# Modulation products of a three-part network: from TensorE to GpSimd, during the feed-forward layers

## What is computed

```python
def conv_glu_ffn(x, w_up, conv_w, conv_b, w_down):
    h = causal_depthwise_conv(x @ w_up, conv_w, conv_b)
    gate, val = jnp.split(h, 2, axis=-1)
    return (jax.nn.silu(gate) * val) @ w_down
# first part, twice: h = h + mixer(rmsnorm(h)); h = h + conv_glu_ffn(rmsnorm(h))
# then, for each of the 2 hybrid layers and for both c (latents) and c_ctx (context):
#   mod = silu(c) @ w_mod[layer] + b_mod[layer]     # 1024 -> 3072
```

## Time and profile before

| | |
|---|---|
| device time, median of 3 runs | 2967.27 us (2965.48 to 2967.45) |
| span of the profiled execution | 2965.5 us (its device time 2965.48 us) |
| TensorE matmuls | 2901.6 us busy, 98% |
| TensorE weight loads | 2393.2 us, 81% |
| VectorE | 1477.4 us, 50% |
| ScalarE | 1163.9 us, 39% |
| GpSimd | 146.0 us, 5% |
| mean granted clock of TensorE | 0.997 |
| DMA | 260.98 MB, mean 88 GB/s |

### The profile page before, as it was taken

The page is one execution under the profiler, slowest core; times in us unless marked ns, Lnnn a source line. Parts: engine busy times, 40 slices in busy tenths (PEclk is TensorE's granted clock), DMA queues, the critical chain, the costliest instruction groups (busy, mean ns, idle before and its releaser), DMA issues.

```text
span 2965.5 us, 38348 instructions
## 1 busy us (share of the span) xinstructions
PE 2901.6 (98%) x15438; PEld 2393.2 (81%) x15438; DVE 1477.4 (50%) x2051; ACT 1163.9 (39%) x1856; POOL 146.0 (5%) x199
## 2 busy tenths in 40 slices
PE   9999999999999999999999999999999999999998
PEld 7778888776788887877888788868888788888776
DVE  5655455546463657366252543263455735453454
ACT  5444333526452344146233431173232743341452
POOL 1000000110000000100000300100001000200100
PEclk9999999999999999999999999999999999999999
DMA  5343332331332222210112221311113022321322
GB/s 185 122 158 105 113 128 85 129 130 38 136 107 98 99 87 76 82 54 22 60 43 76 85 68 57 101 60 64 57 64 101 21 82 78 108 91 66 121 75 85
DMA packets 48844, 260.98 MB, mean 88 GB/s; under 512 B 6872, under 2 KB 7904, under 8 KB 24896
## 3 DMA queue, kind: packets, MB, share of 16 engines
q1 hardware_dynamic: 36288, 213.75, 20.8%
q0 software_dynamic: 12416, 45.25, 4.5%
HBM read 250.50 MB, written 4.28 MB: 86 GB/s over the span
## 4 chain that ended last, share of the span: by engine, by line
PE 91%; DVE 4%; ACT 3%; DMA 1%; issue 1%; POOL 0%; SPq 0%; DVEq 0%; ACTq 0%
PE PS L897 15%; PE PS L898 15%; PE PS L899 15%; PE PS L874 7%; PE PS L876 7%; PE PS L875 7%; PE PS L833 3%; PE PS L835 3%; PE PS L834 3%; PE PS L1124 2%; PE PS L1086 1%; PE PS L1197 1%; PE PS L1179 1%; PE PS L1166 1%; PE PS L944 1%
## 5 line engine op out<-in xcount | busy, mean ns | idle before, releaser
L897 PE MATMUL PS<-HHX,WHX 128*128 128x512 f32 (+1 forms) x1440 | 504.6, 350 | 0.4 <-DVE WLX L2409 0.3
L898 PE MATMUL PS<-HL,WHX 128*128 128x512 f32 (+1 forms) x1440 | 503.4, 350 | 0.0
L1680 ACT ACTIVATE WHX<-W 128x2048 fp32r<-128x2048 f32 (+1 forms) x102 | 174.8, 1713 | 560.9 <-DMA W<-in_w 379.2
L899 PE MATMUL PS<-HHX,WLX 128*128 128x512 f32 (+1 forms) x1008 | 350.1, 347 | 0.0
L2409 DVE TENSOR_TENSOR WLX<-W,WHX 128x2048 fp32r<-128x2048 f32 x60 | 137.5, 2292 | 344.9 <-ACT WHX L1680 344.8
L897 PEld LDWEIGHTS PS<-HHX,WHX 128*128 128x128 f32 x1440 | 272.7, 189 | 38.3 <-DVE WLX L2409 1.5
L898 PEld LDWEIGHTS PS<-HL,WHX 128*128 128x128 f32 x1440 | 272.7, 189 | 34.9
L874 PE MATMUL PS<-HH,WH 128*128 128x512 f32 x672 | 261.7, 389 | 0.0
L876 PE MATMUL PS<-HH,WL 128*128 128x512 f32 x672 | 261.7, 389 | 0.0
L875 PE MATMUL PS<-HL,WH 128*128 128x512 f32 x672 | 261.6, 389 | 0.0
L2409 DVE TENSOR_TENSOR WL<-W,WH 128x2048 fp32r<-128x2048 f32 x68 | 155.7, 2290 | 177.8 <-ACT WH L1680 177.7
(11 more groups left out here) (553 smaller groups left out, 5813.8 us busy)
## 6 DMA issues: line engine op xcount, KB each, us to landing
W<-in_w SPq DMA_DIRECT2D x172, 1024.0 KB, 4.8
XC<-in_wm POOLq DMA_DIRECT2D x12, 1024.0 KB, 5.2
H<-in_wm POOLq DMA_DIRECT2D x12, 1024.0 KB, 6.0
W<-in_wb SPq DMA_DIRECT2D x24, 512.0 KB, 3.3
W<-in_w SPq DMA_DIRECT2D x8, 768.0 KB, 4.1
ARENA<-ARENA POOLq DMA_DIRECT2D x32, 128.0 KB, 2.3
ARENA<-mrow SPq DMA_DIRECT2D x12, 256.0 KB, 3.9
PR<-in_nbias POOLq DMA_DIRECT2D x12, 256.0 KB, 3.0
```

The source lines that it names most:

```text
L897: pe.matmul(dst, wh[:, s, c], hi[:, k, t0:t1], start=k == 0, stop=False)
L898: pe.matmul(dst, wh[:, s, c], lo[:, k, t0:t1], start=False, stop=False)
L899: mm = pe.matmul(dst, wl[:, s, c], hi[:, k, t0:t1], start=False, stop=k == kb - 1)
L1680: act.activation(dst[:, s, 0:n], W[:, s, 0:n], ACT.Copy).then_inc(wh_ready[s], 1)
```

## The change

The eight matmuls for each slab go away, with SCW, the zeroing of PSUM and the count `mods`. In their place GpSimd multiplies, in the stage "up" at the head of each feed-forward layer, slabs 0 to 15 (first layer) and 16 to 23 (second layer), one behind the other. For one slab and each of its 8 row blocks it does two multiplications of 128x256 by a per-partition scalar (silu(c), silu(c_ctx)), into the slab's row of MACC or into one of two 128x512 buffers (RST and PR); from the second row block on, an addition of 128x512 sums them. That is 16 multiplications and 7 additions. Each instruction counts `mod_step` up, and GpSimd waits on that count: before the products of row block k (k from 2) for everything issued, before the last addition for everything issued, and before it issues the load of slab i+2 for the whole slab i. The sum over the 128 partitions is left to TensorE: in the third "down" of the first layer and in the second "down" of the second layer it waits until GpSimd has finished the group, and then does one matmul of 512 columns per slab, with a stationary operand of 32 columns out of ONEHOT of which one is all ones (16 and 8 matmuls, four at a time in four column groups). ScalarE copies the rows out, TensorE sums and turns them with four matmuls, VectorE adds `b_mod`, as before but once per group.

```diff
+MOD_GROUPS = (0, 16, MODS)
+    MACC = ARENA[:, split_at + 4 * KT * SLAB + KT * T:][:, 0:16 * 2 * SLAB].rearrange("p (a b) -> p a b", a=16)
+    MODP = PR[:, 0:4 * P]
-    def pe_mod(pe, st, n, done=0):
-            pe.wait_ge(mod_loaded[i % 2], 16 * (i // 2 + 1))
-                    mm = pe.matmul(PS[32 * g:32 * g + MOD_COLS, 4 + i % 2, 0:SLAB], SCW[:, c:c + MOD_COLS],
-                                   mod_slab(i)[:, k, :], start=opens and half == 0, stop=half == 1,
-                                   skip_group_check=True)
-            mm.then_inc(mod_used, 1)
...
+    def mod_steps(slabs):
+        return (3 * KT - 1) * slabs
+    def mod_group(st):
+        if st.kind == "down" and (st.layer, st.step0) == (0, PARTS[0] + PARTS[1]):
+            return 0
+        if st.kind == "down" and (st.layer, st.step0) == (1, PARTS[0]):
+            return 1
+        return None
+    def pool_mod(pool, own, i):
+        row = i - MOD_GROUPS[int(i >= MOD_GROUPS[1])]
+        acc = MACC[:, row, :].rearrange("p (c n) -> p c n", c=2)
+        made = [RST[:, T:2 * T], MODP]
+        pool.wait_ge(mod_loaded[i % 2], 16 * (i // 2 + 1))
+        def product(k):
+            dst = made[k % 2].rearrange("p (c n) -> p c n", c=2) if k else acc
+            wait(pool, mod_step, own.n - (1 if k < 2 else 0))
+            for c in range(2):
+                own.mark(pool.tensor_scalar(dst[:, c, :], mod_slab(i)[:, k, :], SC[:, k, c:c + 1], None, ALU.mult))
+        def add(k):
+            pool.wait_ge(mod_step, own.n - (2 if k + 1 < KT else 0))
+            own.mark(pool.tensor_tensor(acc, acc, made[k % 2].rearrange("p (c n) -> p c n", c=2), ALU.add))
+        product(0)
+        product(1)
+        for k in range(1, KT):
+            if k + 1 < KT:
+                product(k + 1)
+            add(k)
+    def pe_mod_rows(pe, group):
+        first, end = MOD_GROUPS[group:group + 2]
+        pe.wait_ge(mod_step, mod_steps(end))
+        wait(pe, sem("mod_out"), group)
+        for j in range((end - first) // 4):
+            for g in range(4):
+                mm = pe.matmul(PS[32 * g:32 * g + 32, 4, :], ONEHOT[:, 3 - j:3 - j + 32], MACC[:, 4 * j + g, :],
+                               start=j == 0, stop=4 * j + 4 == end - first, skip_group_check=True)
+        mm.then_inc(sem("mod_rows"), 1)
...
     def pe_down(pe, st):
-        if takes_ctx(st):
-            pe_mod_sum(pe, 1, 3)
-        pe_mod(pe, st, min(st.mods, 1))
+        group = mod_group(st)
+        if group is not None:
+            pe_mod_rows(pe, group)
...
         pe_split_unit(pe, st, 0, tile_of(HIDH), tile_of(HIDL), (hid_lo, ready), kb=st.n, slots=(1,))
+        if group is not None:
+            pe_mod_sum(pe, group)
...
     def act_down(act, own, st):
-        if st["mod"] + st.mods == MODS and st.mods:
-            act_mod_out(act, 0, 2, MODS - 1)
+        group = mod_group(st)
+        if group is not None:
+            act_mod_out(act, group)
...
     @block.gpsimd
-            for i in range(st["mod"] + 2, min(st["mod"] + st.mods + 2, MODS)):
-                pool.wait_ge(mod_used, i - 1)
-                if st.kind in ("units", "tok"):
-                    pool.wait_ge(w_ready[1], 16 * (st["it"] + i - st["mod"]))
-                pool.dma_start(mod_slab(i), wm[i, :, :, :]).then_inc(mod_loaded[i % 2], 16)
+            if st.kind == "up" and st.step0 == 0:
+                pool.wait_ge(h_ready, st["hr"])
+                pool.wait_ge(sem("sc_ready"), 1)
+                wait(pool, sem("mod_rows"), st.layer)
+                for i in range(*MOD_GROUPS[st.layer:st.layer + 2]):
+                    pool_mod(pool, own, i)
+                    if i + 2 < MODS:
+                        pool.wait_ge(mod_step, mod_steps(i + 1))
+                        pool.dma_start(mod_slab(i), wm[i + 2, :, :, :]).then_inc(mod_loaded[i % 2], 16)
```

More of the change, by code:

```diff
@@ L152, in plan_stages @@
     norm("H", "load", "mix0_norm")
-    units(["xa", "ga"], at="H", era="even", split=True, first=True, mods=2)
+    units(["xa", "ga"], at="H", era="even", split=True, first=True)
     add("lru", {**full(0, 1, 2, 3, n=2), **free(0, 1, 2, 3, n=2)})
-    units(["cp", "vb", "bp"], at="H", era="even", split=True, mods=3)
-    units(["res", "res"], at="Y", era="even", split=True, final=True, mods=1)
-    norm("H", "res", "ffn_norm0", mods=2)
+    units(["cp", "vb", "bp"], at="H", era="even", split=True)
+    units(["res", "res"], at="Y", era="even", split=True, final=True)
+    norm("H", "res", "ffn_norm0")
     for f in range(2):
@@ L163, in plan_stages @@
             add("down", {"it": 2, "ws": 2, "w8": 4, **full(0, 2, n=2), **free(0, 1, 2, 3, n=2)}, layer=f,
-                n=2 * n, step0=sum(PARTS[:part]), split=True, apart=True, final=part == len(PARTS) - 1,
-                mods=((2, 2, 1), (2, 0, 0))[f][part])
+                n=2 * n, step0=sum(PARTS[:part]), split=True, apart=True, final=part == len(PARTS) - 1)
         if f == 0:
-            norm("H", "down", "mix1_norm", mods=2)
-            units(["u", "q", "k"], at="H", era="odd", split=True, first=True, mods=3)
-            tok(["g", "v"], era="odd", split=True, final=True, mods=1)
+            norm("H", "down", "mix1_norm")
+            units(["u", "q", "k"], at="H", era="odd", split=True, first=True)
+            tok(["g", "v"], era="odd", split=True, final=True)
             add("sgu", {**full(0, 1, 2, 3), **free(0, 1, 2, 3)})
@@ L172, in plan_stages @@
             add("fox", {**full(0, 2, n=8), **free(0, 2, n=8), **full(4, n=16), **free(4, n=16)}, jobs=jobs)
-            assert base["mod"] == MODS_EVEN
-            units(["res", "res"], at="Y", era="odd", split=True, first=True, final=True, mods=1)
-            norm("H", "res", "ffn_norm1", mods=2)
+            units(["res", "res"], at="Y", era="odd", split=True, first=True, final=True)
+            norm("H", "res", "ffn_norm1")
     norm("both", "down", "final_norm")
@@ L682, in pe_mod_sum, with act_mod_out @@
+    def pe_mod_sum(pe, group):
+        pe.wait_ge(sem("mod_out"), group + 1)
+        wait(pe, sem("mod_saved"), group)
+        for b in range(4):
+            mm = pe.matmul(PS[:, 5, 16 * b:16 * b + 16], MODP[:, b * P:(b + 1) * P],
+                           PC[:, PCOL["mod_sum"]:PCOL["mod_sum"] + 16], start=True, stop=True,
                            skip_group_check=True)
         mm.then_inc(sem("mod_summed"), 1)
[L685 to L689, removed]
+    def act_mod_out(act, group):
+        act.wait_ge(sem("mod_rows"), group + 1)
+        wait(act, sem("mod_summed"), group)
+        act.activation(MODP, PS[:, 4, :], ACT.Copy).then_inc(sem("mod_out"), 1)
@@ L691, in dve_mod_save @@
     def dve_mod_save(dve, group):
[L693 to L703, removed]
-                              ALU.add).then_inc(sem("mod_saved"), 1)
+        dve.wait_ge(sem("mod_summed"), group + 1)
@@ L706, in pe_idle, with slabs_of @@
+        i0, i1 = MOD_GROUPS[group:group + 2]
+        def slabs_of(v):
+            return v.rearrange("p (a m c) -> p a m c", m=2, c=2)[:, i0:i1, :, :]
+        new = PS[:, 5, 0:64].rearrange("p (c m a) -> p a m c", m=2, c=2)[:, 0:i1 - i0, :, :]
+        dve.tensor_tensor(slabs_of(MODT[:, :, :, :].rearrange("p a b c -> p (a b c)")), new,
+                          slabs_of(PC[:, PCOL["b_mod"]:PCOL["b_mod"] + 4 * MODS]),
+                          ALU.add).then_inc(sem("mod_saved"), 1)
     def pe_idle(pe, n):
@@ L1735, in act_down @@
             if u == 0:
-                if st["mod"] + st.mods == MODS and st.mods:
-                    act_mod_out(act, 1, 3, MODS)
                 if takes_ctx(st):
@@ L3036, in _ @@
     def _(pool):
+        own = Own(pool, mod_step)
         pool.memset(EPSC[:, 0:1], EPS).then_inc(consts, 1)
@@ L3256, in pad8 @@
         return o
+    mod_sum = np.zeros((P, 16), np.float32)
+    for slab in range(16):
+        mod_sum[32 * (slab % 4) + slab // 4, slab] = 1.0
     ffn = []
```

75 lines of the change are left out of this document (19 added, 56 removed).

## The result

The changed kernel takes 3147.03 us in the median of 4 runs (3143.95 to 3147.68), beside 2967.36 us for the kernel before on the same chip: ratio 1.0604, 95% interval 1.0589 to 1.0619. It is slower by 180 us, where +22 was forecast and the range ended at 3030. The direction was right, the size was not.

A forecast was written before the change was run, and what follows sets the result against it. TensorE, busy 98% of the span, was taken as the bound. Terms -19.8 + 6 + 29 (waiting for GpSimd) + 4 + 1 + 2 gave +22 us on 2967.3, so 2989 us, range 2954 to 3030 us.

The forecast's parts named there:

- Slabs off TensorE, row matmuls on: TensorE's stream: 18 exposed slabs removed, -19.8 us, 24 new matmuls of 512 columns, +6 us; together -13.8 us.
- The multiplication: GpSimd's 128x256 product by a scalar: 0.40 us each, bounds 0.29 and 0.73, 6.4 us a slab.
- the 21: GpSimd's first group: 21 us of its 277 pass under VectorE's time, 12 of waits and issue, 9 of start-up.
- The room and the lock: GpSimd's first group: 325 us from start to deadline, less 98 us lost to VectorE's two-SBUF-input operations, leaves 227 us.
- The waits on its own count: GpSimd waiting for its issued instructions, eight times a slab: 0.2 us each, bounds 0.1 and 0.3, 1.6 us a slab.
- the other count: First group: if VectorE's L2462 operations were locked out too, room shrinks by 64 us and TensorE waits 93 us.
- Group 1: GpSimd's slabs in the second feed-forward layer: 128 us needed in a room of 149, no wait, 21 us to spare.
- VectorE: VectorE's two-input operations delayed by GpSimd in the feed-forward layers: +4 us, bounds 0 and 12.
- The clock: Granted clock falling after TensorE's waits: +1 us for the three norms, +2 us behind the long wait.
- 17 us with little work: Profile stretch before a granted clock of 0.88 over 11 us, read as 1.3 us' worth of work lost.
- The dear multiplication: GpSimd's multiplications cost 0.73 us like a two-input operation; TensorE waits 113 and 21 us: 3096 us, chance 10%.
- VectorE as the bound: Feed-forward layers: VectorE's six two-input operations a unit each wait a whole addition, +33 us besides the wait: 3022 us, 8%.

The follow-up runs named there:

- kernel with the filled norms: Ten matmuls on constants added in each of the three norms that lost slabs, against the changed kernel cut to one column an operation: 2953.58 us.
- kernels with one column: Changed kernel with each GpSimd multiplication and addition working on one column of each half, MACC zeroed once per group: 2958.02 us, ratio 0.9971.
- kernel without reads: Changed kernel with GpSimd's instructions replaced by memsets of about the same time, plus a MACC memset ahead of each group: 3039.79 us.
- paired multiplication: Changed kernel with each row block's two multiplications by a scalar made one two-input multiplication of 128x512: 3016.97 us, ratio 1.0171.
- kernel that follows: Kernel before, with 18 slabs moved to GpSimd using one two-input multiplication per row block, six norm slabs kept on TensorE: 2954.66 us, ratio 0.9961.

## Why the prediction was wrong

The terms can be checked against one point, TensorE's first waiting matmul in the fourth norm (before: 1161.58 us), behind which neither kernel has any of this work. The kernel with the filled norms is there at 1146.29: the pure gain of the edit on TensorE is 15.3 us. The changed kernel is there at 1338.74, +177.2. The terms: waits 182.8; gain -15.3; norms at half clock +5.4 (taken from the kernels with one column, without and with the filling); the two rounds of row matmuls 5.8 + 3.4, against 3.6 + 1.9 = 5.5 in the filled kernel, +3.7. Sum 176.6, and 0.6 us are left for VectorE. Behind the point the changed kernel takes 1806.3 us and the kernel before 1803.9; the others lie between 1803.1 and 1805.6, so these 2.4 us are no term of the edit that I can name. The same sum for the kernel without reads, whose first row matmuls take 5.4 us, gives 80.8 - 15.3 + 5.4 + 1.8 = 72.7, measured +72.5. For the paired multiplication (5.3 us) it gives 46.2 - 15.3 + 5.4 + 1.7 = 38.0, measured +45.5, so 7.5 are left. Of these, 3.4 are its longer waits before L957, and two of these waits, 1.16 and 0.72 us at 284 to 286 us, stand in front of a stretch at half clock (mean 0.61 and 0.54 in the next two windows of 2 us) which the other kernels don't have there. The rest is not attributed.

- **Slabs off TensorE, row matmuls on.** -13.8 forecast, -15.3 measured with the norms filled. Right; some 1.6 of the 15.3 are clock and not slabs, since the stretch at half clock of the earlier trace rows (706 to 710 us) is missing in the filled kernel. The changed kernel has one like it at 846 to 852 us; in return its stretch behind the second norm costs 1.5 us where that of the one-column kernel costs 2.8, so the sum above stands. In the changed kernel the first norm's matmul comes at 181.46 instead of 187.04 us, 5.6 for the six exposed slabs before it.
- **The multiplication.** This step failed: the price of one multiplication on GpSimd. 0.40 us was forecast with bounds 0.29 and 0.73, 0.91 measured, above both. The 0.40 came from a copy, and the bounds from other operations too (a select on half the columns, a two-input addition), and I took for granted that an operation with one input lies below one with two. It costs one and a half times the two-input one of the same width. With 0.91 in the prediction's own sum the slab comes to 25.5 us, 16 of them to 408; less the 21 and the room of 227 that makes 160, measured 148. For group 1 it is 204 - 10 - 149 = 45, measured 34.6. So this one term explains the miss: the waits are 183 us where 29 were forecast, 154 more, and the time is 158 us above the forecast. I had written that 0.1 us on it moves the wait by 26 us, and it was off by 0.5.
- **The room and the lock.** Right within 8 us. TensorE came to the row matmuls 324 us after GpSimd's start (189.5 to 513.6), where 325 was forecast. The sharing with VectorE costs 69 us of the first wait (worked out above), where the prediction took 98 - 21 = 77. VectorE's operation with an input in PSUM stayed at 744 ns, as the Trainium skill (SBUF — State Buffer, Who interferes with whom) has it; the other count, with that operation locked out too, would have added 64 us to the wait, and there is no room for them.
- **The waits on its own count.** 0.2 us each forecast, 0.1 measured, which was the lower bound. With additions that are 0.03 longer a slab took 25.2 us instead of the 25.5 of the sum above: 5 us in 16 slabs. With the 8 us of the lock, less the 1 us of the room, that is the 12 us between 160 and 148.
- **Group 1.** No wait forecast, 34.6 us came, for the same reason; I had written that its slack is gone at 0.6 us a multiplication, and a wait there was one of the signs of being wrong.
- **VectorE.** +4 forecast, 0.6 left over in the changed kernel, and 4 to 7.5 us in those with the paired form (3.7 by its waits in the kernel that follows), where VectorE's low parts of the hidden values took twice as long (1681 ns instead of 836). No run tells why the slow ones disturb less.
- **The clock.** +3 forecast. 5.4 us behind the norms, and 3.7 us on the row matmuls: three times the size, with the sign right. The 3.4 us too many for VectorE cancel half of this, which is luck. TensorE had stood still before the row matmuls, and the granted clock was 0.50 in the long wait (515 to 662 us), which is 1.2 GHz, and stayed there for most of the row matmuls. Here are the windows behind the wait, and the same row matmuls in the filled kernel:

```profile
662.00:668.00 6.00, 6.00 (x34) 1.46 (x27) 0.00 (x0) 0.25 (x1) 0.97 (x1) 0.63 0.56 175
668.00:672.00 4.00, 4.00 (x19) 3.31 (x18) 0.00 (x0) 0.35 (x1) 0.00 (x0) 1.00 0.01 4
...
512.40 3.64 PE L695 MATMUL PS<-ARENA,ONEHOT 128*32 128x512 f32 x32
```

The prediction also read its one example of such a stretch poorly: in the "17 us with little work" before TensorE was busy 13.1 us.
- **The rivals.** The dear multiplication (10%) is the one that came, with the place and the mechanism as described: 113 and 21 us there, 148 and 35 here, and 3096 against 3147, because its price was an upper bound that did not bound. The Trainium skill (GPSIMD Engine Reference, Engine selection) calls one-input operations roughly line-rate. The runs speak against it here: 0.91 us for 256 columns is four times the 0.21 us that the prediction estimated by that page, and even the copy takes twice that. VectorE as the bound is refuted by the sum above, which leaves it 0.6 us, and by the wait before L957, which stayed at 1.0 us.

What stays open: why the multiplication by a scalar is slower a column than the two-input one. The runs show that it is, at 256 and 512 columns, and that reading the scalar is no more than 85 ns of it.

## What to carry to other kernels

Price an operation by a row of that very operation; where there is none, a bound borrowed from another kind is no bound, and the range must say so. When work moves to an idle engine, compare its length with the room between its start and its deadline, and not its share of the span; the shortage then stands in full as a wait of the engine that was the bound. What stands in an unavoidable wait of TensorE may be worth leaving there, since it keeps the clock up.

## What the runs showed of the hardware

- GpSimd, 32-bit floats, 128 partitions, 256 columns: memset 0.31 us, copy 0.40, two-input multiplication with a broadcast scalar 0.62, multiplication by a constant 0.84, by a per-partition scalar 0.93. At 512 columns: two-input multiplication with both inputs read by zero strides 1.04 us, addition of two full inputs 1.26, multiplication by a scalar 1.57.
- A GpSimd instruction without reads (a memset) neither delayed VectorE's two-input operations (2290 ns) nor was delayed by them (25.0 us a slab beside VectorE, 24.9 without it).
- How much VectorE loses depends on which instructions GpSimd sends: the low part of the hidden values took 836 ns beside multiplications by a scalar and additions, and 1681 ns beside two-input multiplications and additions.
- Behind a wait of 3.0 us in a norm, TensorE worked for some us at 1.2 GHz (granted clock 0.61 over 4 us); with 2.4 us of matmuls on constants in that wait it stayed at 2.4 GHz, and three such places brought 4.4 us.
